# Attention values with the values stationary and the probabilities moving, and the softmax division ahead of the transposition

## The reference

```python
z = rms_norm(x, g_mix) @ w_in + b_in          # columns q | k | v | u | v_gate
s = jnp.where(band_mask, q_block @ k_blocks.T * HEAD_DIM ** -0.5, -inf)
m = max(max(s), sink)
e = exp(s - m)
probs = e / (sum(e) + exp(sink - m))          # the sink column is dropped
out = probs @ v_blocks
x = x + concat(out, gm_out) @ w_out + b_out
```

## Time and profile before

| | us |
|---|---|
| median of 3 runs | 996.93 (996.17 to 998.24) |
| the profiled execution, its own time | 998.08 |
| its span in the profile | 996.3 |
| TensorE busy | 971.6 |
| VectorE busy | 673.2 |
| ScalarE busy | 456.6 |
| GpSimd busy | 278.3 |
| VectorE busy, 442 to 462 us | 11.03 of 20 |
| ScalarE busy, 442 to 462 us | 11.32 of 20 |
| VectorE busy, 485 to 497 us | 10.77 of 12 |

### The profile page before, as it was taken

The page is one execution under the profiler, slowest core; times in us unless marked ns, Lnnn a source line. Parts: engine busy times, 40 slices in busy tenths (PEclk is TensorE's granted clock), DMA queues, the critical chain, the costliest instruction groups (busy, mean ns, idle before and its releaser), DMA issues.

```text
span 996.3 us, 19264 instructions
## 1 busy us (share of the span) xinstructions
PE 971.6 (98%) x7965; PEld 956.7 (96%) x7965; DVE 673.2 (68%) x999; ACT 456.6 (46%) x742; POOL 278.3 (28%) x155
## 2 busy tenths in 40 slices
PE   6999999999999999999999999999999999999996
PEld 5999999999999999999989999999999999999995
DVE  5799657856768563456875399757756758755575
ACT  6644424532544444555434455434543444445132
POOL 2303202211111226321448412301311111215461
PEclk9999999999999999999999999999999999999998
DMA  7952433252243327221114693243324224234202
GB/s 213 165 122 73 129 96 104 67 159 66 63 128 106 96 75 206 76 64 43 44 54 128 127 170 96 75 127 96 96 87 126 85 64 138 79 111 140 73 14 86
DMA packets 192178, 101.38 MB, mean 102 GB/s; under 512 B 13018, under 2 KB 189492, under 8 KB 192076
## 3 DMA queue, kind: packets, MB, share of 16 engines
q1 hardware_dynamic: 176624, 90.76, 32.1%
q0 software_dynamic: 11440, 5.77, 4.7%
q10 hardware_dynamic: 4028, 3.63, 1.2%
HBM read 97.59 MB, written 3.59 MB: 102 GB/s over the span
## 4 chain that ended last, share of the span: by engine, by line
PE 89%; DVE 5%; DMA 2%; ACT 2%; POOL 1%; issue 1%; SPq 0%; DVEq 0%; ACTq 0%
PE ps L1612 52%; PE ps L1692 32%; DMA w_raw<-in_w_ffn_dram 1%; PE ps L1648 1%; POOL h_lo L1061 1%; PE ps L1929 1%; DMA x_rows<-in_x_prompt_dram 1%; PE ps L1902 1%; DVE ab L1325 0%; ACT w_hi L693 0%; ACT h_hi L800 0%; PE ps L1643 0%; DVE mix_lo L1499 0%; DVE rs_t L1143 0%; DVE xb_lo L1177 0%
## 5 line engine op out<-in xcount | busy, mean ns | idle before, releaser
L1692 PE MATMUL ps<-xo_lo,w_hi 128*128 128x260 f32 x1008 | 284.7, 282 | 0.0
L1692 PE MATMUL ps<-xo_hi,w_lo 128*128 128x260 f32 x1008 | 284.4, 282 | 0.0
L1692 PE MATMUL ps<-xo_hi,w_hi 128*128 128x260 f32 x1008 | 284.2, 282 | 0.0
L1612 PE MATMUL ps<-h_hi,w_hi 128*128 128x260 f32 x960 | 195.8, 285 | 2.0 <-POOL h_lo L1061 1.2
L1612 PE MATMUL ps<-h_lo,w_hi 128*128 128x260 f32 x960 | 193.6, 283 | 0.0
L1612 PE MATMUL ps<-h_hi,w_lo 128*128 128x260 f32 x960 | 193.6, 283 | 0.0
L1692 PEld LDWEIGHTS ps<-xo_hi,w_lo 128*128 128x128 f32 x1008 | 189.8, 188 | 0.0
L1692 PEld LDWEIGHTS ps<-xo_lo,w_hi 128*128 128x128 f32 x1008 | 189.7, 188 | 0.0
L1692 PEld LDWEIGHTS ps<-xo_hi,w_hi 128*128 128x128 f32 x1008 | 189.6, 188 | 0.0
L1054 POOL TENSOR_TENSOR w_lo<-w_a,w_hi 128x512 fp32r<-128x512 f32 x36 | 66.8, 1857 | 307.6 <-ACT w_hi L762 307.6
L1612 PEld LDWEIGHTS ps<-h_hi,w_hi 128*128 128x128 f32 x960 | 148.2, 189 | 3.6 <-issue 3.4
(11 more groups left out here) (253 smaller groups left out, 1436.5 us busy)
## 6 DMA issues: line engine op xcount, KB each, us to landing
w_raw<-in_w_ffn_dram SPq DMA_DIRECT2D x88, 256.0 KB, 3.0
w_a<-in_w_ffn_dram SPq DMA_DIRECT2D x36, 512.0 KB, 4.9
w_raw<-in_w_ffn_dram SPq DMA_DIRECT2D x48, 384.0 KB, 3.5
w_raw<-in_w_ffn_dram SPq DMA_DIRECT2D x16, 512.0 KB, 6.1
w_lo<-in_w_ffn_dram POOLq DMA_DIRECT2D x11, 512.0 KB, 9.4
w_raw<-in_w_in_dram SPq DMA_DIRECT2D x10, 512.0 KB, 4.0
w_raw<-in_w_ple_gate_dram SPq DMA_DIRECT2D x8, 512.0 KB, 3.9
x_rows<-in_x_prompt_dram SPq DMA_DIRECT2D x4, 512.0 KB, 5.5
```

What stands on the lines that cost most here:

```text
L1612: ins = pe.matmul(ps[:, bank + step * h, 0:HALF], w[:, c, w0:w0 + P], m_[:, sk, h * HALF:(h + 1) * HALF], start=(first and n == 0), stop=( ...
L1692: ins = pe.matmul(ps[:, b, 0:Q], w[:, c, k * P:(k + 1) * P], m_[:, op, k, :], start=(first and k == 0 and n == 0), stop=(k == 3 and n == 2 ...
```

## The change

The stages of an item get new places and new content:

| stage | before | after |
|---|---|---|
| `p_scale` (VectorE) | sums and reciprocal at `p_turn` 0, unit 5+i step 1 | sums, reciprocal and four multiplications of `probs`, unit 5+i step 3 |
| `p_turn` 0 | step 1 | step 3 |
| `p_turn` 1 | step 3 | step 5 |
| `values` | step 5, probabilities stationary | step 7, 64 columns of `v_rows` stationary, 128 columns of `probs_t` moving, the two key heads into partitions 0 to 63 and 64 to 127 of bank 7 |
| multiplication by one over the sum | on the output | on the probabilities, ahead of their transposition |
| `o_turn` / `o_take` | unit 6+i step 1, with two transpositions | unit 6+i step 1, only the two takes, from bank 7 |

`p_turn` r now waits for the scaled probabilities of block r (`probs_scaled`) where it waited for the exponentials. `values` of item i waits for the low take of item i-2 where it waited for that of item i-1. The order of the list within unit 5+i becomes: `o_take(i-1)` before step 1; `scores(i+1)`, `p_scale(i)`, `p_turn(i, 0)` and the gelu's middle before step 3; `soft(i+1)` before step 4; `p_turn(i, 1)` before step 5; `values(i)` before step 7.

```diff
@@ mixer_steps
     for i, u in enumerate(ITEM_UNIT):
         put(u, 3, ("scores", i))
         put(u, 4, ("soft", i))
-        put(u + 1, 1, ("p_turn", i, 0))
-        put(u + 1, 3, ("p_turn", i, 1))
-        put(u + 1, 5, ("values", i))
-        put(u + 2, 1, ("o_turn", i))
+        put(u + 1, 3, ("p_scale", i), ("p_turn", i, 0))
+        put(u + 1, 5, ("p_turn", i, 1))
+        put(u + 1, 7, ("values", i))
+        put(u + 2, 1, ("o_take", i))
@@ ScalarE
-                elif kind == "o_turn":
+                elif kind == "o_take":
                     i = arg[0]
-                    act.wait_ge(o_turned, i + 1)
-                    nc.scalar.activation(mix_hi[:, i // 2, 256 * (i % 2):256 * (i % 2) + 256], ps[:, 7, 256:512],
-                                         ACT.Copy).then_inc(o_hi, 1)
+                    part = slice(256 * (i % 2), 256 * (i % 2) + 256)
+                    act.wait_ge(o_made, i + 1)
+                    nc.scalar.activation(mix_hi[:, i // 2, part], ps[:, 7, part], ACT.Copy).then_inc(o_hi, 1)
@@ VectorE
-                elif kind == "p_turn" and arg[1] == 0:
+                elif kind == "p_scale":
                     i = arg[0]
                     c0 = 16 * (i % 2)
...
                     link(nc.vector.reciprocal(st[:, c0 + 12:c0 + 16], st[:, c0 + 12:c0 + 16]))
-                elif kind == "values":
-                    i = arg[0]
-                    c0 = 16 * (i % 2)
-                    dve.wait_ge(o_made, i + 1)
-                    if i:
-                        dve.wait_ge(o_turned, i)
-                    nc.vector.tensor_tensor(
-                        o_rows[:], ps[:, 7, 0:256].rearrange("p (b c d) -> p b c d", b=2, c=NKV),
-                        st[:, c0 + 12:c0 + 16].rearrange("p (c b) -> p b c", c=NKV).unsqueeze(3)
-                        .broadcast_to([P, 2, NKV, HD]), ALU.mult).then_inc(o_taken, 1)
-                elif kind == "o_turn":
+                    for r in range(2):
+                        for c in range(NKV):
+                            item = probs[:, i % 2, c, r, 0:keys(i % 2, r)]
+                            at = c0 + 12 + 2 * c + r
+                            ins = nc.vector.tensor_scalar(item, item, st[:, at:at + 1], None, ALU.mult)
+                        ins.then_inc(probs_scaled, 1)
+                elif kind == "o_take":
...
-                    nc.vector.tensor_tensor(mix_lo[:, i // 2, part], ps[:, 7, 256:512],
+                    nc.vector.tensor_tensor(mix_lo[:, i // 2, part], ps[:, 7, part],
                                             mix_hi[:, i // 2, part].bitcast(F32), ALU.subtract).then_inc(o_lo, 1)
@@ TensorE
                 elif kind == "p_turn":
                     i, r = arg
-                    pe.wait_ge(exp_done, 5 * (i + 1))
+                    pe.wait_ge(probs_scaled, 2 * i + r + 1)
...
                     pe.wait_ge(probs_taken, 2 * i + 2)
-                    if i:
-                        pe.wait_ge(o_lo, i)
+                    if i >= 2:
+                        pe.wait_ge(o_lo, i - 1)
                     for r in range(2):
                         b = 2 * bp + r
                         ks = (0,) if b == 0 else (0, 1)
-                        for c in range(NKV):
-                            for k in ks:
-                                ins = pe.matmul(ps[:, 7, r * P + c * HD:r * P + (c + 1) * HD], probs_t[:, r, c, k, :],
-                                                v_rows[:, max(b - 1, 0) + k, c * HD:(c + 1) * HD],
-                                                start=(k == 0), stop=(k == ks[-1]))
+                        q0 = 256 * bp + r * P
+                        for k in ks:
+                            for c in range(NKV):
+                                part = slice(c * HD, (c + 1) * HD)
+                                ins = pe.matmul(ps[part, 7, q0:q0 + P], v_rows[:, max(b - 1, 0) + k, part],
+                                                probs_t[:, r, c, k, :], start=(k == 0), stop=(k == ks[-1]))
                     ins.then_inc(o_made, 1)
-                elif kind == "o_turn":
-                    i = arg[0]
-                    pe.wait_ge(o_taken, i + 1)
-                    for r in range(2):
-                        ins = turn(ps[:, 7, (2 + r) * P:(3 + r) * P], o_rows[:, r].rearrange("p c d -> p (c d)"))
-                    ins.then_inc(o_turned, 1)
```

More of the change, by code:

```diff
@@ L402, in hybrid_decoder_layer @@
             lnb = sb("lnb", [P, GM], scope=s)
-            o_rows = sb("o_rows", [P, 2, NKV, HD], scope=s)
             mask = sb("mask", [P, 2, 2 * W], scope=s)
@@ L489, in hybrid_decoder_layer @@
         probs_taken = sem("probs_taken")
-        o_made, o_taken = sem("o_made"), sem("o_taken")
-        o_turned, o_hi, o_lo = sem("o_turned"), sem("o_hi"), sem("o_lo")
+        probs_scaled = sem("probs_scaled")
+        o_made, o_hi, o_lo = sem("o_made"), sem("o_hi"), sem("o_lo")
         spatial_made, spatial_taken = sem("spatial_made"), sem("spatial_taken")
```

## The result

The changed kernel takes 1028.2 us (median of 5 runs, 1027.9 to 1029.2) against 998.2 of the kernel before on the same chip (996.2 to 999.4): ratio 1.0298, 95% interval 1.0286 to 1.031. So it is 30 us slower; 1030 was forecast. The profiled span went from 996.3 to 1027.4 us.

A forecast was written before the change was run, and what follows sets the result against it. TensorE, at work 98% of the span, was taken to bound the kernel. Units 5 to 12 cost 30.0 us, less 3.8 at the tail, plus 6.7 for the clock: +32.9 on 996.9, forecast 1030, range 1009 to 1043.

The forecast's parts named there:

- The second turn's place: ScalarE copies the second turn behind the next exponentials and weight split; values wait 3.35 us in even units, 2.06 in odd.
- Scaling on the path: VectorE's four new multiplications ahead of the first turn; TensorE waits 0.63 us in unit 7, 0.57 in units 6 and 8.
- Units 10 and 11: Norm statistics, small instructions or the sample's softmax come before scaling; net losses of 4.85 and 5.4 us.
- the old 1.5 of slow work: Loss at 0.50 clock behind the earlier kernel's 2.3 us wait ahead of group 2's spatial mixing; expected to go.
- the bound of 12: Upper bound in us for the clock term, 8 x 1.5; the term itself was 6.7, lower bound 0.
- Savings: TensorE work saved per item: turns back 0.22 us, turns behind the scores 0.15, values 0.22 or 0.34.
- sum by units: New waits less saved TensorE work, added over mixer units 5 to 12: 30.0 us.
- Unit 12: Small instructions, five norms and 1.2 us of GpSimd precede scaling: ready at 8.0 against 2.16, net loss 5.1 us.
- Tail: Behind unit 12 the old 2.3 us stop ahead of the spatial mixing and 1.5 behind it go: -3.8 us.
- only the copy's place costs: Rival: VectorE's idle time absorbs scaling, values run fast, clock does not fall; +12, 1009 us; chance 0.12.
- No fall of the clock: Rival: TensorE's clock stays up behind the new waits; +26.2, 1023 us; chance 0.22.
- Faster: Rival: the second turn's copy is there before TensorE reaches the values; 987 us; chance 0.03.

The follow-up runs named there:

- filling: Matmuls nobody reads put where TensorE waits: added to the changed kernel, 1024.1 us; added to the old content at late places, 1019.0 us.
- the unscaled kernel: Changed kernel without the four scalings: 1020.3 us at its late places (the 19.5 us of waits), 991.2 us at the old places (the 10 us comparison).
- the best order: Changed kernel with scaling at step 1 ahead of the previous item's take, turns before steps 3 and 4 (second ahead of exponentials), values before step 6: 1000.4 us.

## Why the prediction was right

| unit | predicted: first turn, values | measured |
|---|---|---|
| 5 | 0.84, 3.35 | 0.61, 3.03 |
| 6 | 0.57, 2.06 | none, 1.45 |
| 7 | 0.63, 3.35 | 0.57, 3.01 |
| 8 | 0.57, 2.06 | none, 1.51 |
| 9 | 0.9, 3.35 | 0.80, 3.03 |
| 10 | 3.5, 2.06 | 3.26, 0.19 |
| 11 | 2.7, 3.35 | 1.13, 3.03 |
| 12 | 5.85, none | 6.50, none |

- *The second turn's place*: right, as mechanism and in the length of its chain; its waits came out 0.3 to 0.6 shorter than forecast (unit 10 apart). Two experiments show it by moving nothing but that turn and its copy: 15 us of the changed kernel, 28 of the old content at late places. The chain from the mask to the values is 5.79 long (444.82 to 450.61) against 5.85.
- *Scaling on the path*: right as a wait of 0.6 in even units and 3 to 6.5 in units 10 and 12; an instruction of 128 elements takes about 0.27 (forecast 0.23), of 256 about 0.35 (0.32). In units 6 and 8 the wait is missing, since work at the lower clock brought TensorE to the turn later. In unit 6 the scaled pair was ready some 4.0 behind the unit's start, as forecast, and TensorE came at 5.1 in place of 3.5: the g turns took 1.05 in place of 0.60 us, and three k steps 3.3 in place of 2.2.
- *Units 10 and 11*: the values' wait of unit 10 was 0.19 and not 2.06, the first turn's of unit 11 was 1.13 and not 2.7. The prediction had no fall of the clock in the work ahead of these two waits. Behind unit 10's first wait a turn and two k steps took 3.5 us (485.23 to 488.69) in place of 1.9. In unit 11, with the clock at 0.50 from 496 to 498 us, TensorE reached the turn 5.0 behind the unit's start in place of 3.3, while the scaling was ready at 6.0 as forecast. This is slow work in the place of a wait.
- *Waits against clock*: both mis-sized, in opposite directions. The prediction had 35.1 us of waits, and 6.7 less the old 1.5 of slow work: 40.3. Measured were 28.1 and 12.6: 40.7. Slow work that fills what would be a later wait moves time from one column to the other, so the split was wrong and the sum right; that the two errors were of the same size is in part luck. By windows of one us, TensorE worked slow for some 6 us behind unit 5's wait, 3.5 behind unit 7's, 3 each in units 10 and 11, 3.5 across the start of unit 12 and 9.6 behind unit 12's wait. That is 29 in all and half of it lost (14.5, an estimate, above the bound of 12 that the clock was given; the kernel before lost 1.7). The forecast had 1.5 lost behind unit 12's wait, where 4.8 were, 1.3 in unit 9, where nothing was, and nothing in unit 10 and ahead of unit 11's first turn. What filling gives back, 4 or more, is near the net 5.2.
- *Savings*: 7.6 us by the groups (8 by experiment), 5.0 in the prediction's sum by units (its 35.1 of waits less 30.0; with the eighth turn back, which the sum leaves out, 5.2). The term at fault is the values: 0.88 and 1.10 where 1.06 and 1.39 were forecast. The row by which I placed them, the scores, was the wrong neighbour. This is most of the 3 us by which the forecast increase (32.9) was above the measured one (30.0). The forecast time was nearer, 1030 against 1028.2, because it was counted from 996.9, where the kernel before took 998.2 beside the changed one: a piece of luck.
- *Unit 12*: ready at E + 9.7, not 8.0. I gave GpSimd 1.2 us (bound 1.75); it held the first pair back by 3.0 (ready at about 520.09, against 516.12 + 0.97). TensorE was 1.1 later too, so the wait grew by 0.65 only.
- *Tail*: the 2.3 ahead of the spatial mixing went, as forecast.
- The rival "only the copy's place costs", at 1009, was mis-sized by far: the move alone gives 1032, and 1020 with the new content unscaled. It took absorbed waits for free time and left out the clock: its 19.5 us of waits are what the unscaled kernel has, and its time was still 11 us short of that kernel's. The forecast was not hurt, because the two costs hide each other. "No fall of the clock" is out by the windows. "Faster" needed a second copy ahead of TensorE, and is what ran only without the scaling and at the old places (991).

What stays open: why the clock did not fall behind unit 9's wait, and how the 10 us between the best order and the unscaled kernel divide between the scaling, its wait in unit 12 (3.9) and the order itself.

## What to carry to other kernels

Where one written order feeds all the engines, moving a stage later for one engine moves its copies behind long work on another: follow the moved stage through each queue before counting what it saves. Costs that make the same engine wait do not add, so test them as a grid (content by place), not one by one. When the busy engine stalls, count its clock in the work behind the stall, but only as far as no later wait would have taken that time anyway (filling the waits gave back 4 us in one kernel here and 13 in another).

## What the runs showed of the hardware

**GpSimd holds up VectorE's scalings, and several operations in a row hold up several of them.** Changed kernel, VectorE and GpSimd, units 5 and 12:

```profile
415.09 3.18 DVE L1441 TENSOR_SCALAR probs<-probs,st 128x128 f32<-128x128 f32 x4
...
516.12 1.21 DVE L1434 TENSOR_TENSOR st<-st 128x4 f32<-128x4 f32 x1
...
517.58 4.10 DVE L1441 TENSOR_SCALAR probs<-probs,st 128x256 f32<-128x256 f32 x4
```

```profile
415.11 2.37 POOL L1032 TENSOR_TENSOR w_lo<-w_raw,w_hi 128x1024 fp32r<-128x1024 f32 x1 [8.35 <-ACT w_hi L692]
...
514.46 2.86 POOL L1102 TENSOR_TENSOR gv_rows<-g_rows,lng 128x512 f32<-128x512 f32 x1 [4.82 <-DVE g_rows L1464]
517.39 1.26 POOL L1104 TENSOR_TENSOR gv_rows<-gv_rows,lnb 128x512 f32<-128x512 f32 x1
518.61 1.31 POOL L1102 TENSOR_TENSOR gv_rows<-g_rows,lng 8x512 f32<-8x512 f32 x1
520.00 1.26 POOL L1104 TENSOR_TENSOR gv_rows<-gv_rows,lnb 8x512 f32<-8x512 f32 x1
```

In unit 5 the scaling and the subtraction start within 0.02 us of each other. Looked at one by one, the first scaling takes 2.46 us (0.27 elsewhere) and ends 0.07 behind the subtraction (417.48); the other three follow in 0.7 us. In unit 12 a small sum (0.15 elsewhere) takes 1.21 and ends with GpSimd's first operation (517.33 and 517.32). Four scalings (1.14 with GpSimd idle) then take 4.10, while GpSimd runs three further operations one right behind the other: the first three scalings take 1.23, 1.35 and 1.42, each to about the end of one of GpSimd's operations, and the fourth, with GpSimd done, 0.34. The Trainium skill (SBUF — State Buffer, SBUF: two separate sides) has the pair of ports that both engines share as a lock, which one of them holds for a whole instruction; for VectorE it says so of instructions in a two-port mode or with two inputs in SBUF. These durations agree with that.

**The clock does not follow the length of a wait alone.** Waits of 3.03, 3.01 and 3.03 us ahead of the values in units 5, 7 and 11 had a stretch at half clock around them, the one of 3.03 in unit 9 had none (1.00 in its window). Neither had those of 1.45 and 1.51. In unit 11 the clock was 0.50 from 496 to 498 us, though TensorE had stood idle for only 0.2 us since 485.23; the 16 matmuls of the sample with 8 moving columns each (491.94 to 493.89) came before it.
